# Expert gates computed beside tiles 48 to 111 of the first expert table, instead of in a stage of their own

## The reference, cut to what matters

```python
s_top, i_top = lax.top_k(s, PEER_TOPK)          # per token, head and side: the 16 best of 128 keys
best, pos = lax.top_k(cand, PEER_TOPK)          # per token and head: the 16 best of 16 x 16 sums
idx = take_along_axis(cand_idx, pos)            # cand_idx = i_top[side 0] * 128 + i_top[side 1]
g = softmax(best)
ue = take(u_tab, idx)
a = gelu(einsum('thkd,td->thk', ue, x))         # 128 picked experts for each token
ve = take(v_tab, idx)
out = einsum('thk,thkd->td', g * a, ve)
```

## Time and profile before

| what | us |
|---|---|
| median of three executions | 2182.33 (2180.05 to 2183.22) |
| the profiled execution, first to last instruction (span) | 2178.2 |
| what lies around the span, taken as median less span | 4.1 |
| TensorE busy | 2004.4 (92%) |
| DVE busy | 1396.6 (64%) |
| ACT busy | 1154.6 (53%) |
| POOL busy | 538.8 (25%) |

### The profile page before, as it was taken

The page is one execution under the profiler, slowest core; times in us unless marked ns, Lnnn a source line. Parts: engine busy times, 40 slices in busy tenths (PEclk is TensorE's granted clock), DMA queues, the critical chain, the costliest instruction groups (busy, mean ns, idle before and its releaser), DMA issues.

```text
span 2178.2 us, 42941 instructions
## 1 busy us (share of the span) xinstructions
PE 2004.4 (92%) x12792; PEld 1811.3 (83%) x12792; DVE 1396.6 (64%) x2629; ACT 1154.6 (53%) x2284; POOL 538.8 (25%) x415
## 2 busy tenths in 40 slices
PE   7899998999966899999998999999999669999997
PEld 5779998999965787888777899989999557878886
DVE  4645897445489765666547459964444996656665
ACT  3344554555567555555533445545555775555554
POOL 5430794000056200000053308930000561000000
PEclk9999999999999999999989999999999999999999
DMA  5215455555500357555522354455555004565555
GB/s 198 78 59 177 152 165 164 183 182 183 182 31 0 108 192 248 183 193 193 183 76 70 97 166 148 166 169 183 183 178 182 7 0 135 193 240 193 192 192 182
DMA packets 90463, 326.96 MB, mean 150 GB/s; under 512 B 10400, under 2 KB 11168, under 8 KB 89760
## 3 DMA queue, kind: packets, MB, share of 16 engines
q1 hardware_dynamic: 90400, 326.18, 45.6%
HBM read 325.09 MB, written 1.05 MB: 150 GB/s over the span
## 4 chain that ended last, share of the span: by engine, by line
PE 79%; DVE 9%; POOL 4%; issue 4%; DMA 1%; ACT 1%; DVEq 1%; SPq 0%; POOLq 0%; ACTq 0%
PE ps L790 11%; PE ps L792 11%; PE ps L791 11%; PE ps L846 10%; PE ps L848 10%; PE ps L849 10%; POOL onehot L1213 2%; DVE x_lo L1550 2%; DVE work L1579 2%; PE ps L821 2%; PE ps L760 1%; PE ps L763 1%; PE ps L762 1%; POOL tab_lo L1200 1%; DVE work L1309 1%
## 5 line engine op out<-in xcount | busy, mean ns | idle before, releaser
L790 PE MATMUL ps<-x_lo,tab_hi 128*128 128x256 f32 x2048 | 581.6, 284 | 18.8 <-POOL tab_lo L1200 18.8
L791 PE MATMUL ps<-x_hi,tab_hi 128*128 128x256 f32 x2048 | 579.5, 283 | 0.0
L792 PE MATMUL ps<-x_hi,tab_lo 128*128 128x256 f32 x2048 | 579.5, 283 | 0.0
L1563 DVE TENSOR_TENSOR tab_lo<-raw,tab_hi 128x512 fp32r<-128x512 f32 x512 | 354.0, 692 | 283.0 <-ACT tab_hi L1126 274.3
L1049 ACT ACTIVATE tab_hi<-raw 128x512 fp32r<-128x512 f32 x504 | 317.7, 631 | 363.5 <-PE ps L792 363.5
L846 PE MATMUL ps<-tab_lo,w_hi 128*128 128x512 f32 x1024 | 401.3, 392 | 12.2 <-DVE w_lo L1599 12.2
L790 PEld LDWEIGHTS ps<-x_lo,tab_hi 128*128 128x128 f32 x2048 | 393.0, 192 | 21.9 <-POOL tab_lo L1200 21.7
L1533 DVE TENSOR_TENSOR tab_lo<-raw,tab_hi 128x512 fp32r<-128x512 f32 x352 | 243.3, 693 | 257.3 <-ACT tab_hi L1049 255.1
L849 PE MATMUL ps<-tab_hi,w_lo 128*128 128x512 f32 x1024 | 400.7, 391 | 0.0
L848 PE MATMUL ps<-tab_hi,w_hi 128*128 128x512 f32 x1024 | 400.6, 391 | 0.0
L791 PEld LDWEIGHTS ps<-x_hi,tab_hi 128*128 128x128 f32 x2048 | 393.1, 192 | 0.0
(11 more groups left out here) (200 smaller groups left out, 2516.5 us busy)
## 6 DMA issues: line engine op xcount, KB each, us to landing
raw<-tab_u SPq DMA_DIRECT2D x256, 512.0 KB, 3.3
raw<-tab_v SPq DMA_DIRECT2D x256, 512.0 KB, 3.3
raw<-w_proj SPq DMA_DIRECT2D x68, 512.0 KB, 3.6
raw<-w_proj SPq DMA_DIRECT2D x16, 384.0 KB, 3.1
work<-cdft SPq DMA_DIRECT2D x3, 1536.0 KB, 10.3
work<-cfilter SPq DMA_DIRECT2D x3, 768.0 KB, 5.6
work<-sub_keys SPq DMA_DIRECT2D x2, 1024.0 KB, 6.2
work<-pmat SPq DMA_DIRECT2D x3, 352.0 KB, 7.0
```

Of the source, the lines that this page charges most:

```text
L790: mm(bank, hi, x_lo[:, 4 * h + k, :], start=(h + k == 0), stop=False)
L791: mm(bank, hi, x_hi[:, 4 * h + k, :], start=False, stop=False)
L792: last = mm(bank, lo, x_hi[:, 4 * h + k, :], start=False, stop=(h + k == 4))
L1563: v.tensor_tensor(half(tab_lo, s, h), half(raw, s, h), half(tab_hi, s, h).bitcast(F32), ALU.subtract).then_inc(lo_dve.sem, 1)
```

## The change

The separate gate stage is gone. Its 64 groups are placed behind tiles 48 to 111 of the first table, one group behind each tile.

- POOL sets `work` for tiles 48 to 127 to one: a first piece of 7,936 elements a partition once the normalised input has been transposed, and, once the top-k is done, two pieces of 12,544 together. In each it starts with a 128-element product of ones. Its scaling of the row side is gone. It makes the lower parts of tiles 0 to 39 as before and of tiles 48 to 111 as well.
- TensorE transposes the picks after tile 47, now waits for their copies at once (`picksT_done`), and then does tile, gates, tile, gates. Before a pair of tiles it waits for `gated` of two pairs before, in place of `gelu_done`.
- DVE makes the row side in one step, four `tensor_scalar` calls of 128x128 a group (compare with one pointer operand, multiply by another), and the column side of every second group. It multiplies the gates into `work`, as before for each group (`weigh_group`). New is `gate_pair`: for the 40 pairs from tile 48 on it multiplies the GELU in PSUM into `work`.
- ACT writes the GELU of those pairs in place in PSUM, and makes the column side of every second group in 32 instead of 48 rounds, between the upper parts. |index - j| has its own buffer `dist_abs`.
- The SP queue waits on `lo_pool` in place of `lo_dve` for the tiles whose lower parts POOL makes; it issues the same DMAs.

The diff, cut to its core:

```diff
+UNIT_A = SPEC + 2048
...
-LO_POOL = 2 * (O0 + 8) + 2 * EARLY
+GATE0, GROUPS = 48, 64
+GATE1 = GATE0 + GROUPS
+LO_POOL = 2 * (O0 + 8) + 2 * EARLY + 2 * GROUPS
 LO_DVE = 2 * TILES - LO_POOL
...
-    with sp.Fori(EARLY // 4 + 1, 32) as i:
+    with sp.Fori(EARLY // 4 + 1, GATE0 // 4 + 1) as i:
         stream(i, tab_u, lo_dve, LO_U)
+    with sp.Fori(GATE0 // 4 + 1, GATE1 // 4 + 1) as i:
+        stream(i, tab_u, lo_pool, LO_G)
+    with sp.Fori(GATE1 // 4 + 1, 32) as i:
+        stream(i, tab_u, lo_dve, LO_T)
...
+    def gates(i, s, first):
+
+        n = i * 4 + s - GATE0
+        pe.wait_ge(*at(hot_i, l, n + 1))
+        pe.wait_ge(*at((hot_j_act, hot_j_dve)[s % 2], l, i * 2 + s // 2 - GATE0 // 2 + 1))
+        if not first:
+            pe.wait_ge(*at(weighted, l, n - 3))
+        for t in range(4):
+            last = mm(ps[:, 2 + s, t * P:(t + 1) * P], onehot[:, s % 2, 0, t, :],
+                      onehot[:, s % 2, 1, t, :], start=True, stop=True)
+        last.then_inc(gates_ready.sem, 1)
+
+    def u_gates(i, first=False):
+        for s in range(4):
+            if s % 2 == 0:
+                if first:
+                    pe.wait_ge(*at(gelu_done, l, i * 2 + s // 2 - 1))
+                else:
+                    pe.wait_ge(*at(gated, l, i * 2 + s // 2 - 1 - GATE0 // 2))
+            u_tile(i, s, lo_pool, LO_G)
+            gates(i, s, first)
+
+    def u_tail(i):
+        for s in range(4):
+            if s % 2 == 0:
+                pe.wait_ge(*at(gated, l, i * 2 + s // 2 - 1 - GATE0 // 2))
+            u_tile(i, s, lo_dve, LO_T)
...
-    def gates(i, first):
-        for s in range(4):
-            n = i * 4 + s
-            pe.wait_ge(*at(hot_scaled, l, n + 1))
-            if s < 3:
-                pe.wait_ge(*at(hot_j_act, l, i * 3 + s + 1))
-            else:
-                pe.wait_ge(*at(hot_j_dve, l, i + 1))
-            if not first:
-                pe.wait_ge(*at(weighted, l, n - 3))
-            for t in range(4):
-                last = mm(ps[:, 2 + s, t * P:(t + 1) * P], onehot[:, s % 2, 0, t, :],
-                          onehot[:, s % 2, 1, t, :], start=True, stop=True)
-            last.then_inc(gates_ready.sem, 1)
-
-    gates(0, True)
-    with pe.Fori(1, 16) as i:
-        gates(i, False)
-
     pe.wait_ge(*at(picksT_done, l, 1))
+    u_gates(GATE0 // 4, first=True)
+    with pe.Fori(GATE0 // 4 + 1, GATE1 // 4) as i:
+        u_gates(i)
+    with pe.Fori(GATE1 // 4, 32) as i:
+        u_tail(i)
...
+    def gelu_in_place(n, bank):
+        act.wait_ge(*at(half_used, l, n * 4 + 2 * U0 + 4))
+        fn(ps[:, bank, :], ps[:, bank, :], ACT.Gelu).then_inc(gelu_done.sem, 1)
+    def distances(i, s, first):
+        q = i * 2 + s // 2 - GATE0 // 2
+        if not (first and s == 0):
+            act.wait_ge(*at(hot_j_act, l, q))
         for t in range(4):
+            last = fn(dist_abs[:, t, :], iota, ACT.Abs,
+                      bias=minus_j[:, bass.ds(i * 16 + 4 * s + t - 4 * GATE0, 1)])
         last.then_inc(abs_done.sem, 1)
+    def one_hot_j(i, s, first):
+        if not (first and s == 0):
+            act.wait_ge(*at(gates_ready, l, i * 4 + s - GATE0 - 1))
+        act.wait_ge(*at(abs_done, l, i * 2 + s // 2 - GATE0 // 2 + 1))
+        fn(onehot[:, 0, 1, :, :], dist_abs[:, :, :], ACT.Relu, scale=-1.0, bias=1.0).then_inc(hot_j_act.sem, 1)
+    def gate_quad(i):
+        distances(i, 0, False)
+        u_upper(i, 0)
+        one_hot_j(i, 0, False)
+        u_upper(i, 1)
+        gelu_in_place(i * 2 - 1, 1)
+        distances(i, 2, False)
+        u_upper(i, 2)
+        one_hot_j(i, 2, False)
+        u_upper(i, 3)
+        gelu_in_place(i * 2, 0)
...
+    u_upper(GATE0 // 4, 0)
+    u_upper(GATE0 // 4, 1)
+    gelu(GATE0 // 2 - 1, 1)
     act.wait_ge(*at(picksT_done, l, 1))
+    distances(GATE0 // 4, 0, True)
+    one_hot_j(GATE0 // 4, 0, True)
+    distances(GATE0 // 4, 2, True)
+    u_upper(GATE0 // 4, 2)
+    one_hot_j(GATE0 // 4, 2, True)
+    u_upper(GATE0 // 4, 3)
+    gelu_in_place(GATE0 // 2, 0)
+    with act.Fori(GATE0 // 4 + 1, GATE1 // 4) as i:
+        gate_quad(i)
...
+            if first and s == 0:
+                gelu_in_place(63, 1)
...
+    def set_ones(start, end):
+        tt(area(start, P), ones, ones, ALU.mult)
+        return nc.gpsimd.memset(area(start + P, end - start - P), 1.0)
+    pool.wait_ge(*at(xT_ready, l, 8))
+    set_ones(UNIT_A, CAND).then_inc(unit_set.sem, 1)
     with pool.Fori(0, EARLY // 4) as i:
         u_lower(i)
-
-    def scale_hot(i, first=False):
-
-        for s in range(4):
-            n = i * 4 + s
-            if s >= 2 or not first:
-                pool.wait_ge(*at(gates_ready, l, n - 1))
-            pool.wait_ge(*at(hot_i, l, n + 1))
-            tt(onehot[:, s % 2, 0, :, :], hot_rows[:, s, :, :].bitcast(F32),
-               picks[:, 2, bass.ds(n * 4, 4)].rearrange("p (t a) -> p t a", a=1).broadcast_to([P, 4, P]),
-               ALU.mult).then_inc(hot_scaled.sem, 1)
-
-    scale_hot(0, True)
-    with pool.Fori(1, 16) as i:
-        scale_hot(i)
+    pool.wait_ge(*at(topk_done, l, 1))
+    set_ones(CAND, P * SEQ).then_inc(unit_set.sem, 1)
+    nc.gpsimd.memset(area(GATE0 * SEQ, UNIT_A - GATE0 * SEQ), 1.0).then_inc(unit_set.sem, 1)
+    with pool.Fori(GATE0 // 4, GATE1 // 4) as i:
+        u_lower(i)
...
+    def hot_rows(n, slot):
+        for t in range(4):
+            last = v.tensor_scalar(onehot[:, slot, 0, t, :], iota, picks[:, 0, bass.ds(n * 4 + t, 1)],
+                                   picks[:, 2, bass.ds(n * 4 + t, 1)], ALU.is_equal, ALU.mult)
+        last.then_inc(hot_i.sem, 1)
+    def hot_columns(n):
+        v.tensor_tensor(onehot[:, 1, 1, :, :], iota.rearrange("p (a c) -> p a c", a=1).broadcast_to([P, 4, P]),
+                        picks[:, 1, bass.ds(n * 4, 4)].rearrange("p (t a) -> p t a", a=1)
+                        .broadcast_to([P, 4, P]), ALU.is_equal).then_inc(hot_j_dve.sem, 1)
+    def weigh_group(n, bank):
+        dve.wait_ge(*at(gates_ready, l, n + 1))
+        cell = work[:, :, bass.ds(n * 4, 4)]
+        v.tensor_tensor(cell, ps[:, bank, :].rearrange("p (t j) -> p j t", t=4), cell, ALU.mult)\
+            .then_inc(weighted.sem, 1)
+    def gate_pair(n, bank, groups):
+        dve.wait_ge(*at(gelu_done, l, n + 1))
+        dve.wait_ge(*at(weighted, l, groups))
+        pair = work[:, bass.ds(2 * n, 2), :]
+        v.tensor_tensor(pair, ps[:, bank, :].rearrange("p (k t) -> p k t", k=2), pair, ALU.mult)\
+            .then_inc(gated.sem, 1)
+    def gate_quad(i, first=False, last=False):
+        for s in range(4):
+            n = i * 4 + s - GATE0
+            if not (last and s == 3):
+                if not (first and s == 0):
+                    dve.wait_ge(*at(gates_ready, l, n))
+                hot_rows(n + 1, (s + 1) % 2)
+                if s % 2 == 0:
+                    hot_columns(n + 1)
+            if s == 0 and not first:
+                gate_pair(i * 2 - 1, 1, n)
+                dve.wait_ge(*at(gated, l, i * 2 - GATE0 // 2))
+            if s == 2:
+                gate_pair(i * 2, 0, n)
+                dve.wait_ge(*at(gated, l, i * 2 + 1 - GATE0 // 2))
+            if last and s == 3:
+                u_lower_half(i + 1, 0, 0)
+                u_lower_half(i + 1, 0, 1)
+            weigh_group(n, 2 + s)
+    hot_rows(0, 0)
+    dve.wait_ge(*at(gelu_done, l, GATE0 // 2))
+    dve.wait_ge(*at(unit_set, l, 3))
+    gate_quad(GATE0 // 4, first=True)
+    with dve.Fori(GATE0 // 4 + 1, GATE1 // 4 - 1) as i:
+        gate_quad(i)
+    gate_quad(GATE1 // 4 - 1, last=True)
+    def tail_quad(i, first=False):
+        for s in range(4):
+            for h in range(2):
+                if s or not first:
+                    u_lower_half(i, s, h)
+            if s % 2:
+                gate_pair(i * 2 + s // 2 - 1, (s // 2 + 1) % 2, GROUPS)
+    tail_quad(GATE1 // 4, first=True)
+    with dve.Fori(GATE1 // 4 + 1, 32) as i:
+        tail_quad(i)
...
+            if first and s == 0:
+                gate_pair(63, 1, GROUPS)
```

More of the change, by code:

```diff
@@ L777, in _, with u_tile @@
                 pe.wait_ge(*at(scores_dve, l, 2))
+                def u_tile(i, s, signal, offset):
+                    j = i * 4 + s
+                    bank = ps[:, s // 2, (s % 2) * 256:(s % 2) * 256 + 256]
+                    for h in range(2):
+                        pe.wait_ge(*at(signal, l, j * 2 + offset + h + 1))
+                        for k in range(4):
+                            col = slice(k * P, (k + 1) * P)
+                            hi, lo = half(tab_hi, s, h)[:, col], half(tab_lo, s, h)[:, col]
+                            mm(bank, hi, x_lo[:, 4 * h + k, :], start=(h + k == 0), stop=False)
+                            mm(bank, hi, x_hi[:, 4 * h + k, :], start=False, stop=False)
+                            last = mm(bank, lo, x_hi[:, 4 * h + k, :], start=False, stop=(h + k == 4))
+                        last.then_inc(half_used.sem, 1)
@@ L779, in u_product @@
```

(36 more changed lines are left out.)

73 lines of the change are left out of this document (18 added, 55 removed).

## The result

The changed kernel takes 2054.89 us (median of four, 2052.14 to 2057.65) against 2181.51 us of the kernel before in the same runs: a ratio of 0.9425 with a 95% interval of 0.9413 to 0.9438. The forecast was 2065 us, with 2052 to 2135 as its range. The profiled execution has a span of 2050.3 us, 127.9 less than before.

What follows compares the result with a forecast made beforehand. TensorE's work plus a gate stage where it mostly waits bound the kernel. Per layer 122.3 - 60.8 - 1.9 - 0.9 = 58.7 us, two layers 117.4, gave 2065 us against 2182.3; range 2052 to 2135.

Steps and rivals of the forecast that it cites:

- What bounds it: Whole layer: TensorE's work bounds both tables; between them lies one gate stage in which TensorE mostly waits.
- Removed, 122.3 us a layer: Gate stage between the tables: 121.0 us goes, and 1.3 us more from the second table's slow beginning.
- A group, 0.95 us, 60.8 a layer: Eight gate records added on TensorE behind each of 64 tiles: 0.95 us each, bounds 0.89 and 1.15.
- Stop after tile 47, 1.9: TensorE waits there for the three copies of the picks: 1.9 us a layer, between 1.4 and 2.5.
- Start of the second table, 0.9: The last pair's GELU and product on ACT and DVE delay tile 1: 0.9 us a layer, between 0 and 2.
- Setting to one, 0, bound 2: POOL's filling of `work` with ones, in two pieces, is hidden or in time: cost 0, at most 2 us.
- The rival by which the memset holds DVE: Tiles 40 to 47 and first piece: memset blocks DVE's lowers, TensorE starves 34 us a layer, 2133 us; 8%.
- Sum: Per layer, removed time less added costs: 122.3 - 60.8 - 1.9 - 0.9 = 58.7 us; two layers 117.4.
- DVE and port at nothing: Tiles 48 to 111: DVE's work and its port shared with POOL cost nothing, covered by 2.3 us slack a pair.
- The rival in which DVE sets the pace: Tiles with gates, POOL's lowers holding DVE: mildly 2093 to 2138 us, 22%; fully 2272 us, slower than before, 5%.
- Groups don't pack: Rival: each gate group on TensorE stands alone, 1.15 plus 0.2 us for a wait; 51 us more, 2116; 9%.
- the change does nothing: Rival: something unseen makes TensorE stand through each gate group as today, so the layer isn't shortened: 2182 us; 2%.

Runs made afterwards that it cites:

- the ramp in PSUM: DVE's row-side and column-side calls read column numbers from PSUM: changed kernel 2054.51 us; with one gate matmul of four 1967.89; with doubled row-side calls 2069.27.
- The moved wait: Changed kernel with TensorE's wait for the copied picks moved from before tile 48 to behind it, ahead of its first gates: 2053.71 us, ratio 0.9413.
- the run with DVE's own lowers: Changed kernel with the lower parts of tiles 48 to 111 made by DVE instead of POOL, one tile ahead: 2091.82 us, ratio 0.959.

## Why the prediction was right

- **What bounds it.** Right: the stage was taken out whole and TensorE has no gap in its place. With the ramp in PSUM, taking 86 us of TensorE's work away gained all of it (1967.89 against 2054.51 us).
- **Removed, 122.3 us a layer.** 121.0 plus 3.27 - 1.84 = 1.4: 122.4.
- **A group, 0.95 us, 60.8 a layer.** Measured 3.77 - 2.88 = 0.89, 56.8 a layer: the dense end of the bounds. The size was off by 4.0 us a layer, 8 of the 10 us by which the forecast was too slow. The 0.06 us that the forecast put on top of the dense pace are not there: nothing is lost where a tile's matmuls and the gates' meet, and the matmuls that read `onehot` have no idle time before them in the changed kernel's trace.
- **Stop after tile 47, 1.9.** From the transposes' end (378.42 + 6 x 0.11) to 380.86: 1.8. The moved wait showed that only part of it can be had by moving.
- **Start of the second table, 0.9.** 671.43 - 670.62 - 0.23 = 0.6. The forecast's own figures, 3.4 against 2.7, give 0.7, not the 0.9 that it used.
- **Setting to one, 0, bound 2.** 0, at a measured 0.85 ns an element. The rate in the Trainium skill that the forecast gives, 1.03 cycles an element (GPSIMD Engine Reference, Elementwise — side-by-side cycle accounting), makes 0.86 ns at the page's 1.2 GHz, an estimate; the trace agrees. The rival by which the memset holds DVE is void, and its mechanism is true for a POOL operation that reads.
- **Sum.** 122.4 - 56.8 - 1.8 - 0.6 = 63.2 a layer, 126.4; the spans differ by 127.9. Of the other 1.5 us the wait at the parameter loads has 0.75 (4.11 us before, 3.36 after, in layer 0); the rest was not taken apart.
- **DVE and port at nothing.** Right for this kernel, and for the first reason given, the phase: weighting, row sides in POOL's rest, column side just ahead of POOL. What the forecast put wrongly is the cover: 2.3 us of slack in a pair. DVE's sum is right (132.69 / 200 x 7.53 = 5.0 us a pair, forecast 5.3), but its slack can't be spent, nor TensorE's pace raised. With 0.67 us less of TensorE's work a tile, which leaves 6.2 us for a pair, the calls ran into the lowers and a tile took 3.8 us. The rival in which DVE sets the pace had 22% plus 5%; the runs show that the changed kernel stands at its edge, at no cost. That the margin was enough is in part luck: the forecast had no measure of how thin it was.
- **Groups don't pack, and the change does nothing.** Both are void: there is no wait on `onehot` in TensorE's list, and no stage is left.

## What to carry to other kernels

A stage bound by a helper engine can be spread beside a stage bound by TensorE. Price it by TensorE's dense rate, and expect the first wait and the new starts to cost something: 1.8 and 0.6 us a layer here. When DVE and POOL are laid side by side, count port time and phases as well as busy time: an engine busy for two thirds can still be the bound as soon as the spacing changes. If a small constant operand is what makes a DVE call meet POOL, try it in PSUM: the call takes 67 ns more here, and in none of these runs was it held.

## What the runs showed of the hardware that was not expected

- Taking away 86 us of TensorE's work gained nothing while calls of 0.33 us stood beside POOL's lowers; with the ramp in PSUM it gained 87 us. The loss sits in DVE's queue and is set off by TensorE's pace, which also sets the spacing of POOL's lowers.
- Two DVE operations of 0.69 us took 21.81 us beside POOL products that read SBUF for 21.69 us, while beside memsets of 6.8 and 3.7 us they took 0.69.
- One `tensor_scalar` of 128x128 with two pointer operands takes 335 ns from SBUF and 402 from PSUM; four in a row from SBUF take 1.11 us where nothing holds them (the run with DVE's own lowers).
